# Attention's product with V: one float32 matmul on probabilities copied once, in place of two float32r matmuls on a split copy

## What is computed

```
o_cmp = einsum('bhgqc,bhcd->bhgqd', pc, vc)        # 31 compressed keys
o_slc = einsum('bhgqnk,bhqnkd->bhgqd', ps, vg)     # selected blocks
o_win = einsum('bhgqk,bhkd->bhgqd', pwin, vwb)     # window
o = g0 * o_cmp + g1 * o_slc + g2 * o_win           # g: sigmoid gates
```

## Time and profile before

| what | us |
|---|---|
| median of 3 runs | 1464.96 |
| lowest and highest run | 1464.4, 1466.36 |
| the profiled execution | 1467.22 |
| its span, first to last instruction | 1465.4 |

### The profile page before, as it was taken

How to read it: one execution, slowest core, us unless ns; L and a number is a source line. 1 busy time by engine, 2 the same in 40 slices (tenths; PEclk the granted TensorE clock), 3 DMA queues, 4 the chain that set the end, 5 groups by cost and what they waited for, 6 DMA issues and landing times.

```text
span 1465.4 us, 19937 instructions
## 1 busy us (share of the span) xinstructions
PE 1385.8 (95%) x6884; PEld 1146.8 (78%) x6884; DVE 724.5 (49%) x1031; ACT 606.3 (41%) x1089; POOL 717.7 (49%) x548
## 2 busy tenths in 40 slices
PE   5999799989999999999999998989999999999997
PEld 4889787768888888888778887866778888888885
DVE  4415547954444444444444055498254444455444
ACT  4224355854533333432352343568364333333321
POOL 4444636873544444344354455468554444444442
PEclk9999898999999999999999999999999999999999
DMA  6332320012322322333133332200123222322321
GB/s 271 101 99 88 116 72 15 1 44 68 102 90 100 100 93 93 101 101 98 60 123 115 100 102 74 85 1 1 62 68 102 92 94 100 100 90 96 101 72 58
DMA packets 34722, 126.41 MB, mean 86 GB/s; under 512 B 3936, under 2 KB 4320, under 8 KB 34272
## 3 DMA queue, kind: packets, MB, share of 16 engines
q1 hardware_dynamic: 34656, 125.53, 25.6%
HBM read 123.42 MB, written 2.10 MB: 86 GB/s over the span
## 4 chain that ended last, share of the span: by engine, by line
PE 83%; DVE 8%; POOL 3%; ACT 3%; issue 2%; DMA 1%; POOLq 0%; SPq 0%; DVEq 0%; ACTq 0%
PE bank L1655 32%; PE bank L1348 19%; PE bank L1688 17%; PE bank L1363 6%; DVE pt_l L919 2%; DVE s_bias L1159 2%; POOL w_lo L537 2%; PE bank L1325 1%; PE bank L1446 1%; PE bank L1622 1%; PE bank L1601 1%; DVE act_lo L919 1%; PE bank L1526 1%; PE bank L1527 1%; PE bank L1547 1%
## 5 line engine op out<-in xcount | busy, mean ns | idle before, releaser
L544 POOL TENSOR_TENSOR w_lo<-raw,w_hi 128x1024 fp32r<-128x1024 f32 x152 | 365.1, 2403 | 456.3 <-ACT w_hi L649 267.4
L1655 PE MATMUL bank<-act_hi,w_hi 128*128 128x512 f32 (+1 forms) x768 | 287.0, 374 | 7.3 <-POOL w_lo L537 7.2
L1655 PE MATMUL bank<-act_hi,w_lo 128*128 128x512 f32 (+1 forms) x768 | 286.1, 372 | 0.0
L1655 PE MATMUL bank<-act_lo,w_hi 128*128 128x512 f32 (+1 forms) x768 | 286.1, 372 | 0.0
L643 ACT ACTIVATE w_hi<-raw 128x1024 fp32r<-128x1024 f32 x132 | 139.5, 1058 | 337.2 <-PE bank L1348 165.2
L537 POOL TENSOR_TENSOR w_lo<-raw,w_hi 128x1024 fp32r<-128x1024 f32 x68 | 164.9, 2436 | 101.8 <-ACT w_hi L643 101.4
L878 ACT ACTIVATE cv<-bank,par 128x512 f32<-128x512 f32 x88 | 68.5, 778 | 285.6 <-PE bank L1655 285.6
L1284 DVE SCALAR_TENSOR_TENSOR cv<-bank,par,cv 128x511 f32<-128x511 f32 x88 | 66.0, 750 | 226.0 <-ACT cv L878 225.8
L1348 PE MATMUL bank<-w_hi,act_hi 128*128 128x512 f32 (+1 forms) x448 | 171.8, 383 | 2.6 <-POOL w_lo L537 2.5
L1655 PEld LDWEIGHTS bank<-act_hi,w_hi 128*128 128x128 f32 x768 | 145.5, 189 | 33.5 <-POOL w_lo L537 8.0
L1348 PE MATMUL bank<-w_lo,act_hi 128*128 128x512 f32 (+1 forms) x448 | 170.3, 380 | 0.0
(11 more groups left out here) (171 smaller groups left out, 2323.8 us busy)
## 6 DMA issues: line engine op xcount, KB each, us to landing
raw<-wstream SPq DMA_DIRECT2D x220, 512.0 KB, 3.5
g_rest<-gains SPq DMA_DIRECT2D x2, 1536.0 KB, 11.5
x<-x_in SPq DMA_DIRECT2D x4, 512.0 KB, 8.1
x_out<-x SPq DMA_DIRECT2D x8, 256.0 KB, 2.0
const<-consts SPq DMA_DIRECT2D x1, 1030.0 KB, 12.5
g_mix_pre<-gains SPq DMA_DIRECT2D x2, 512.0 KB, 5.1
par<-pars SPq DMA_DIRECT2D x2, 235.0 KB, 7.4
const<-consts SPq DMA_DIRECT2D x1, 224.0 KB, 5.4
```

Source lines behind the costliest of these rows:

```text
L544: nc.gpsimd.tensor_tensor(w_lo[:, s, :], raw[:, s, :], r32(w_hi[:, s, :]), ALU.subtract).then_inc(lo_ready, 1)
L1655: last = mm(bank[:, b, first:end], a, v, start=(k == 0 and n == 0), stop=(k == KD - 1 and n == 2), skip_group_check=True)
```

## The change

V is no longer split: ScalarE copies it as float32 (`VF`, 64 columns to a key tile, group and branch), and VectorE's four subtractions and the two instructions for `VcS` are gone. The transposed probabilities are copied once, unrounded, to `pt` with four buffers: even items by ScalarE, odd ones by VectorE. The product is one float32 matmul of 512 columns with 64 stationary columns. The output then lies in 64 partitions: ScalarE rounds it from PSUM into `act_hi` in two instructions, VectorE subtracts for `act_lo` in two; `o_a`, `o_f` and GpSimd's part fall away. The core of the diff:

```diff
-        VS = sb("VS", [P, T, 2 * NKV, 2 * DH], F32R)
+        VF = sb("VF", [P, T, 2 * NKV, DH])
-            pt_h = sb("pt_h", [P, 2, G * P], F32R, att)
-            pt_l = sb("pt_l", [P, 2, G * P], F32R, att)
+            pt = sb("pt", [P, 4, G * P], F32, att)
...
-                def out_rest(v):
-                    i, g = query_tile(v)
-                    dst = (slice(None), slice(4 + 2 * g, 6 + 2 * g), slice(i * P, (i + 1) * P))
-                    pool.wait_ge(oh_done, upto(oh_done, l, v + 1))
-                    nc.gpsimd.tensor_tensor(act_lo[dst], o_f[:], r32(act_hi[dst]), ALU.subtract).then_inc(ol_done, 1)
...
-                def p_round(k):
+                def p_copy(k):
                     rows = NCP if ITEMS[k][0] is None else P
                     act.wait_ge(pt_done, upto(pt_done, l, k + 1))
-                    if k >= 2:
-                        act.wait_ge(pv_done, upto(pv_done, l, k - 1))
-                    nc.scalar.activation(pt_h[0:rows, k % 2, :], bank[0:rows, 3 + k % 3, :], ACT.Copy)\
-                        .then_inc(pth, 1)
+                    if k >= 4:
+                        act.wait_ge(pv_done, upto(pv_done, l, k - 3))
+                    nc.scalar.activation(pt[0:rows, k % 4, :], bank[0:rows, 3 + k % 3, :], ACT.Copy)\
+                        .then_inc(pt_act, 1)
...
-                    minus(VS[:, t, :, DH:2 * DH], bank[:, 4 + t, 0:4 * DH].rearrange("p (a d) -> p a d", a=4),
-                          r32(VS[:, t, :, 0:DH])).then_inc(vg_dve, 1)
...
-                def p_rest(k):
+                def p_copy(k):
                     rows = NCP if ITEMS[k][0] is None else P
-                    dve.wait_ge(pth, upto(pth, l, k + 1))
-                    minus(pt_l[0:rows, k % 2, :], bank[0:rows, 3 + k % 3, :], r32(pt_h[0:rows, k % 2, :]))\
-                        .then_inc(ptl, 1)
+                    dve.wait_ge(pt_done, upto(pt_done, l, k + 1))
+                    if k >= 4:
+                        dve.wait_ge(pv_done, upto(pv_done, l, k - 3))
+                    nc.vector.tensor_copy(pt[0:rows, k % 4, :], bank[0:rows, 3 + k % 3, :]).then_inc(pt_dve, 1)
...
-                        w, rows = VS[:, j, 2 * b + g, :], P
-                    pe.wait_ge(ptl, upto(ptl, l, k + 1))
-                    mm(o, w, pt_h[0:rows, k % 2, :], start=first, stop=False)
-                    mm(o, w, pt_l[0:rows, k % 2, :], start=False, stop=(k == LAST_OF_V[v])).then_inc(pv_done, 1)
+                        w, rows = VF[:, j, 2 * b + g, :], P
+                    copied(k)
+                    mm(o, w, pt[0:rows, k % 4, :], start=first, stop=(k == LAST_OF_V[v])).then_inc(pv_done, 1)
```

More of the change, by code:

```diff
@@ L245, in build @@
         vg_act = sem("vg_act", 8)
[L246 removed]
+        vg_dve = sem("vg_dve", 4)
         inv_ready = sem("inv_ready", 1)
@@ L826, in _ @@
                     y_round(n)
[L829 removed]
+                def p_copy(k):
                     rows = NCP if ITEMS[k][0] is None else P
                     act.wait_ge(pt_done, upto(pt_done, l, k + 1))
[L832 to L841 removed]
+                    if k >= 4:
+                        act.wait_ge(pv_done, upto(pv_done, l, k - 3))
+                    nc.scalar.activation(pt[0:rows, k % 4, :], bank[0:rows, 3 + k % 3, :], ACT.Copy)\
+                        .then_inc(pt_act, 1)
                 def out_round(v):
                     i, g = query_tile(v)
[L845 to L847 removed]
+                    act.wait_ge(pv_done, upto(pv_done, l, LAST_OF_V[v] + 1))
+                    for m in range(2):
+                        view = bank[0:DH, 6 + v % 2, :].rearrange("p (a b c) -> p a b c", a=2, b=2)[:, :, m, :]
+                        nc.scalar.activation(act_hi[m * DH:(m + 1) * DH, 4 + 2 * g:6 + 2 * g, i * P:(i + 1) * P],
+                                             view, ACT.Copy).then_inc(oh_done, 1)
                 for k in range(NI + 4):
@@ L851, in _ @@
                         hi(l, WO_CHUNK_AT[k + 1])
-                    if k < NI:
-                        p_round(k)
+                    if k < NI and k % 2 == 0:
+                        p_copy(k)
                     if k == 1:
@@ L1138, in _ @@
                     minus(KcL[half * DH:(half + 1) * DH, :], kcf[:], r32(KcH[0:DH, :])).then_inc(kc_l, 1)
-                dve.wait_ge(vc_h, upto(vc_h, l, 1))
-                minus(VcS[:, :, DH:2 * DH], vcf[:], r32(VcS[:, :, 0:DH])).then_inc(vc_l, 1)
                 for f in range(2):
@@ L1256, in compressed_step @@
                                                 ALU.mult).then_inc(c_step, 1)
-                for k in range(NI + 3):
+                for k in range(NI + 4):
                     for unit, p in pairs_at(k - 2):
                         factors(unit, p)
-                    if k < NI:
-                        p_rest(k)
+                    if k < NI and k % 2:
+                        p_copy(k)
                     compressed_step(k)
@@ L1584, in _, with copied @@
                     last.then_inc(y_turned, 1)
+                def copied(k):
+                    done = (pt_act, pt_dve)[k % 2]
+                    pe.wait_ge(done, upto(done, l, k // 2 + 1))
                 def turn_p(k):
@@ L1614, in product @@
                     if n is None:
-                        pe.wait_ge(vc_l, upto(vc_l, l, 1))
-                        g = v % NKV
-                        w, rows = VcS[:, g, :], NCP
+                        w, rows = vcf[:, v % NKV, :], NCP
                     else:
                         i, g, b = UNITS[n]
-                        w, rows = VS[:, j, 2 * b + g, :], P
-                    pe.wait_ge(ptl, upto(ptl, l, k + 1))
-                    mm(o, w, pt_h[0:rows, k % 2, :], start=first, stop=False)
-                    mm(o, w, pt_l[0:rows, k % 2, :], start=False, stop=(k == LAST_OF_V[v])).then_inc(pv_done, 1)
+                        w, rows = VF[:, j, 2 * b + g, :], P
+                    copied(k)
+                    mm(o, w, pt[0:rows, k % 4, :], start=first, stop=(k == LAST_OF_V[v])).then_inc(pv_done, 1)
                 for k in range(NI):
```

65 lines of the change are left out of this document (21 added, 44 removed).

## The result

The changed kernel takes 1483.99 us (median of 4 runs, 1483.91 to 1486.5) beside 1465.47 of before: a ratio of 1.0131, 95% interval 1.0113 to 1.0148. It is 18.5 us slower. The forecast was 1466.5 and the range ended at 1474, so the prediction was wrong. The profiled execution has a span of 1484.7 us where before had 1465.4, so 19.3 us have to be found between the two traces.

What follows compares the result with a forecast made beforehand. PE was taken as the bound, with DVE equally full mid-attention. 1464.96 + 3.0 (both attention stages: dearer products less vanished waits) - 1.0 (V's split) = 1467.0, 1465.3 with the low product price; 1466.5 was taken, range 1460 to 1474.

Steps and rivals of the forecast that it cites:

- The product's price (0.87): Attention stage: one float32 product takes 0.87 us of PE against 0.465 for the old two, +19.4 us a layer.
- Its bounds: Product's price: lower 0.853 us from four clocks a column, upper 0.94 us from sixteen times the short record's 59 ns.
- the 59 ns: Distance between `second_layer`'s 64-column float32 records; what stands above their clocks was taken as mostly a fixed few ns a record.
- dearer product: Rival, attention products: four passes at a float32r matmul's price, 0.92 us each product, +4.8, 1471.3 us; chance 0.15.
- Which waits go: Attention stage: the waits for `cE` and `pt_l` and the slow clock after them all go, leaving PE the only bound.
- the prediction's sum, 62.3: PE's work in us, first product to output projection, if it never waits, before the change; 80.7 measured.
- The 0.5 for overlooked waits: Attention stage: 0.5 us added to the sum of 81.7 for overlooked waits, giving 82.2.
- DVE's pace: Attention stage: DVE relieved by 16.3 us a layer, to about 1.2 us an iteration against PE's new 1.78.
- The 18.4: Attention stage before the change: 80.7 - 62.3 = 18.4 us a layer counted as waits and slow clock.
- The sum itself: Attention stage 82.2 against 80.7 us, +1.5 a layer, +3.0 in all; with V's split the kernel comes to 1467.0.
- V's split: Ahead of `z_build`: four DVE subtractions fewer, start about 0.6 us earlier, 0.5 taken twice, -1.0 us; `VcS` 0.
- The rival of the spell at 150: Stall at 149.38 shrinks, slow spell behind it stays out in both layers: -6.8, 1459.7 us; chance 0.15.

Runs made afterwards that it cites:

- the kernels with 128 columns: Changed kernel with 128 stationary columns in the float32 product instead of 64: 1469.22 us; with the compressed items also in all 128 rows: 1466.16 us.
- inside a pair: Changed kernel with the products of two items one behind the other in each odd iteration, none in the even ones: 1478.84 us, ratio 1.0105.
- the kernel with the full array always: Changed kernel with 128 stationary columns and the compressed items padded by zero rows to 128 rows: 1466.16 us, ratio 1.0013.
- The engines' relief at PE's old price: Changed kernel with V, compressed V and probabilities rounded to float32r, rests left out, each product issued twice: 1439.48 us, ratio 0.9829.
- the twelve kernels: All follow-up kernels, variants of the changed kernel or the kernel before, each compared with the kernel before on the same chip: 1439.48 to 1490.98 us.
- the kernel with 32 columns: Changed kernel with 32 stationary columns, half of V's columns left out: 1485.53 us, ratio 1.0141.
- the kernel with 96 columns: Changed kernel with 96 stationary columns, V's 64 and 32 of the columns beside them: 1471.07 us, ratio 1.0051.

## Why the prediction was wrong

- **The product's price (0.87): the step that failed.** It measured 1.10. Of this, 0.86 is the price of a float32 product whose loads are hidden, as the kernels with 128 columns show, so "four clocks a column" was right. The sentence that failed is "The 64 stationary columns instead of 128 save nothing, because the weight load already lies beside the streaming before it". The load does so only between tiles of the same kind. Changing from the full array to 64 columns and back costs 0.24 us: 0.093 ahead of the product, 0.051 between its records, 0.096 behind it. 96 times 0.23 is 22 us. (By the stages it is (92.6 - 80.4) / 48 = 0.25: a further 0.01 shows from the causal mask behind the product to the score after it, 0.038 where the full array has 0.028.)
- **Its bounds** (0.853 to 0.94) didn't reach 1.10, because the row they came from the earlier trace rows shows records among their like, where no change of tile lies. The sign was in the trace of before, at the edges of that same group, which I didn't read:

```profile
187.98 0.39 PE L1363 MATMUL bank<-act_lo,w_hi 128*128 128x512 f32 x1
188.21 0.39 PE L1363 MATMUL bank<-act_hi,w_lo 128*128 128x512 f32 x1
188.53 0.45 PE L1497 MATMUL bank<-hid,par 128*64 128x64 f32 x4
188.90 0.63 PE L1502 MATMUL bank<-par,hid 128*32 128x64 f32 x8
189.46 0.50 PE L1363 MATMUL bank<-act_hi,w_hi 128*128 128x512 f32 x1
```

  The projection's matmuls are 188.21 - 187.98 = 0.23 apart, and the last one ahead of the 64-column group takes 188.53 - 188.21 = 0.32. From the last 64-column record to the first of 32 columns the stamps give 0.152, and from the last of those to the projection 0.149, where records within a group, behind its first gap, are 0.054 to 0.058 apart. That is 0.09 at each change of tile, the figure that the product then showed. The load was there too, inside the group of the earlier trace rows: by the stamps its first two records are 0.080 apart and the others 0.054 to 0.056. So the 59 ns were an average with one exposed load in it, not a fixed few ns a record.
- **The rival "dearer product"** had the right place and too small a size (0.92). Its reason, a fixed addition for each pass, was wrong: inside a pair a record takes 0.429, two clocks for each of 512 columns (0.427) and 2 to 3 ns above.
- **Which waits go: right.** No wait for `cE` or `pt_l` is left, and the clock is 1.00 from 240 on. PE's own work by the prediction's sum, 62.3, and 48 x (1.10 - 0.465) = 30.5 make 92.8; measured are 92.6. That this is so close is partly luck: with every load hidden the same sum gives 62.3 + 48 x (0.86 - 0.465) = 81.3 and 80.4 were measured, so it is some 0.9 too high, and the price of 1.10 is a little low. The 0.5 for overlooked waits was not needed. The step that all this hung on, DVE's pace, is confirmed by its busy time of 27.23 in 45 us, 61% where "some 70%" was forecast; the share is lower since the stage itself runs slower (at the price assumed, in the kernel with the full array always, it is 31.03, 69%). The engines' relief at PE's old price (1439.48 us) was worth 25 us, where two times 18.4 would be 37. The 18.4 was no pure sum of waits: 2.2 of it are the 0.28 us that each of the eight compressed items pays in the kernel before.
- **The sum itself: near enough once the price is right.** With every load hidden the stage takes 80.4 us (forecast 82.2) and the kernel 1466.16 (forecast 1466.5), a ratio of 1.0013. That the two times agree to 0.4 us is luck in part, since the stage was missed by 1.8 us a layer.
- **V's split: right in size, and in mechanism up to PE's stall.** 0.8 at `z_build` and 0.6 at PE; 1.4 us over both layers against 1.0, but very unevenly, 1.3 and 0.1.
- **What was not forecast:** two slow spells in the feed-forward part went. In the kernel before:

```profile
379.10:382.50 3.40, 3.40 (x19) 3.40 (x17) 0.00 (x0) 0.60 (x1) 0.00 (x0) 0.50 0.45 159
```

  and one of the same length at 1099.3. In the kernel after the clock is 1.00 there. Each was worth half of its 3.4 us, 1.7, which is the 1.8 and 1.5 us gained outside the stages. Why they go I did not try, and the change need not be the reason: none of the twelve kernels touches the feed-forward part, and the first spell is there in seven of them (the kernel with 32 columns has it at 387.9, the clock again 0.50), the second in nine. The rival of the spell at 150 did not come: the window's clock is 0.69 as before.

From the forecast of +2 us to the measured +19.3, roughly: 22 for the price, less 1.2 for the stages' sum, less 3.4 for what the outside gained beyond V's split.

## What to carry to other kernels

Read a group of matmuls at its edges, not only inside: the gap ahead of its first record and behind its last is what an instruction pays that stands alone between others. A float32 matmul with 64 or fewer stationary columns among full-array ones was cheaper here when padded to 128 columns and 128 rows, and also when put next to its like. And a relief of one engine that is paid by a full other one should be taken item by item, where the full one waits, not everywhere.

## What the runs showed of the hardware that I had not expected

- With float32, a product with a stationary tile of 32 or 64 columns loses time where it meets a full tile, in two ways. A pause comes at each change, the same for 32 and 64 columns: 0.202 us ahead and 0.525 behind, where 0.109 and 0.429 are had otherwise. And its load lies open, in the gap to its second record. A tile of 96 or 128 columns (and 128 rows) has neither. Between two 64-column tiles nothing is exposed (0.429).
- The exposed load between the two records of a product grows with its columns: 0.027, 0.053, 0.080 and 0.106 us above 0.427 for 32, 64, 96 (32 rows) and 128 (32 rows). The Trainium skill, TensorE: Matmul & The Clock Gate, section LDWEIGHTS (loading the stationary operand), gives the load as its columns divided by 1.2 in ns; the traces agree.
- 32 rows instead of 128 cost 0.28 us an item, with float32 and with float32r (kernel before) alike, though nothing else differs. The Trainium skill, on the same page, section Why this matters for your kernels, says that a single matmul of 32 rows takes the same time as one of 128. In these traces the streaming does; the change of tile around it does not.
- The Trainium skill, on the same page, Part 3, section The mechanism, says in one place that a load overlaps with a running matmul only when their row groups differ (in another it excepts loads into a background weight buffer). No run here bears the first out: full tiles one behind the other have their loads beside the streaming (PEld at 263.23 and 263.77 above).
- Left open: `cE`'s transposes, float32 with 32 columns, stand 0.108 apart and follow full tiles without any loss (in the kernel with 96 columns the product behind them comes after 0.109), and float32r products of 64 columns pay nothing either (0.228 to 0.240 to the next operation, as with 128). So "a change of tile" is a description that fits float32 products and tiles of 32 rows; which property of the instruction decides was not tried, and what PE does in the pause of 0.09 us no run shows.
